# Layer 1's modulation computed in the steps of layer 0's input projection

## The reference

```
for l in range(DEPTH):                                   # DEPTH = 2
    mod = silu(cond) @ mod_w[l] + mod_b[l]               # (1024) x (1024, 6144), for two cond vectors
    sh_a, sc_a, g_a, sh_f, sc_f, g_f = split(mod, 6)
    hn = rms_norm(x, norm_mix_g[l]) * (1 + sc_a) + sh_a
    out = hybrid_mixer(hn) if l == 0 else rec_mixer(hn)  # both begin with a projection of hn
    x = x + g_a * out
    hn = rms_norm(x, norm_ffn_g[l]) * (1 + sc_f) + sh_f
    x = x + g_f * expert_choice_ffn(hn, ...)             # 16 experts, each takes its top tokens
```

## Time and profile before

| what | value |
|---|---|
| median of 3 runs | 4371.22 us (4369.33 to 4372.78) |
| profiled execution, its own time | 4360.98 us |
| its span, first to last instruction | 4359.0 us |
| mean granted clock of TensorE | 0.955 |
| busy in the span: TensorE, VectorE, ScalarE, POOL | 3926.4, 1756.0, 1102.8, 184.5 us |
| stage: `hyena_in`, i = 1 to 3 and its end | about 132.7 to 320 |
| stage: route of layer 0 | 1065.4 to 1166 |
| stage: route of layer 1 | 3351.1 to 3439 |

### The profile page before, as it was taken

How to read it: one execution, slowest core, us unless ns; L and a number is a source line. 1 busy time by engine, 2 the same in 40 slices (tenths; PEclk the granted TensorE clock), 3 DMA queues, 4 the chain that set the end, 5 groups by cost and what they waited for, 6 DMA issues and landing times. The chain is left out here.

```text
span 4359.0 us, 55904 instructions
## 1 busy us (share of the span) xinstructions
PE 3926.4 (90%) x23853; PEld 3152.1 (72%) x23853; DVE 1756.0 (40%) x2865; ACT 1102.8 (25%) x2095; POOL 184.5 (4%) x203
## 2 busy tenths in 40 slices
PE   7999979998499999997999999999687399999995
PEld 4544545553299999996888888888543399999995
DVE  3325457733611111111377887888832511111112
ACT  3110135422011110111354455454422001011111
POOL 1000000000000000000000000000000000000000
PEclk8999999999699999999999999999898699999998
DMA  5311010024978888885101001100224388888884
GB/s 182 106 72 70 16 49 1 1 73 153 312 238 258 264 258 264 256 259 155 41 27 33 28 29 30 32 17 19 98 78 145 115 255 257 263 258 259 257 260 158
DMA packets 515926, 615.14 MB, mean 141 GB/s; under 512 B 16474, under 2 KB 466700, under 8 KB 512992
## 3 DMA queue, kind: packets, MB, share of 16 engines
q1 hardware_dynamic: 492480, 525.18, 37.3%
q0 software_dynamic: 19872, 75.69, 6.3%
q10 hardware_dynamic: 3328, 10.71, 0.6%
HBM read 558.36 MB, written 53.17 MB: 140 GB/s over the span
## 5 line engine op out<-in xcount | busy, mean ns | idle before, releaser
L1671 PEld LDWEIGHTS moe_pgu<-step_hnT,mw_w 128*128 128x128 f32 x8192 | 1117.3, 191 | 16.5 <-issue 16.5
L1671 PE MATMUL moe_pgu<-step_hnT,mw_w 128*128 128x160 f32 x8192 | 1125.0, 300 | 3.4 <-ACT step_hnT L1711 3.4
L1735 DVE TENSOR_TENSOR moe_hT<-moe_sg,moe_pgu 128x160 f32<-128x160 f32 x256 | 82.1, 321 | 1027.4 <-PE moe_pgu L1671 972.0
L1683 PE MATMUL moe_pol<-mw_w,moe_hT 128*128 128x256 f32 x2048 | 457.5, 381 | 2.3 <-DVE moe_hT L1735 1.0
L1922 PE MATMUL rec_pz<-step_hnT,rec_w 128*128 128x256 f32 x1920 | 424.5, 380 | 3.5 <-ACT l_zc L1994 1.9
L1683 PEld LDWEIGHTS moe_pol<-mw_w,moe_hT 128*128 128x128 f32 x2048 | 383.2, 190 | 59.0 <-DVE moe_hT L1735 9.9
L1722 ACT ACTIVATE moe_sg<-moe_pgu 128x160 f32<-128x160 f32 x256 | 77.6, 303 | 1317.8 <-PE moe_pgu L1671 1317.8
L1922 PEld LDWEIGHTS rec_pz<-step_hnT,rec_w 128*128 128x128 f32 x1920 | 362.7, 191 | 52.0 <-ACT l_zc L1994 2.3
L1926 PE MATMUL rec_pz<-rec_w,step_hnT 128*128 128x256 f32 x1280 | 288.1, 384 | 15.1 <-ACT rec_zg L1997 15.1
L1926 PEld LDWEIGHTS rec_pz<-rec_w,step_hnT 128*128 128x128 f32 x1280 | 243.9, 193 | 50.6 <-ACT rec_zg L1997 17.9
L1952 PE MATMUL rec_pg<-rec_ring 128*128 128x128 f32 x1600 | 196.5, 281 | 47.1 <-DVE rec_AT L2249 19.7
(11 more groups left out here) (367 smaller groups left out, 4414.8 us busy)
## 6 DMA issues: line engine op xcount, KB each, us to landing
mw_w<-in_moe_w_gu SPq DMA_DIRECT2D x256, 1024.0 KB, 10.6
mw_w<-in_moe_w_down SPq DMA_DIRECT2D x128, 1024.0 KB, 13.0
mw_w<-in_mod_w SPq DMA_DIRECT2D x24, 1024.0 KB, 14.3
rec_w<-in_r_w_in SPq DMA_DIRECT2D x40, 512.0 KB, 4.0
late_w<-in_mod_w POOLq DMA_DIRECT2D x16, 1024.0 KB, 6.7
scratch_xm<-op_x ACTq DMA_DIRECT2D x20, 512.0 KB, 2.6
scratch_xn<-op_xn POOLq DMA_DIRECT2D x20, 512.0 KB, 5.4
mod_w<-in_mod_w SPq DMA_DIRECT2D x8, 1024.0 KB, 16.5
```

What stands on the lines that cost most here:

```text
L1671: m = nc.tensor.matmul(pgu[2 * (f % 2) + part][:, :], w[:, j, k, (f % 2) * P:(f % 2 + 1) * P], ring[:, k, e % 8, :], start=(k == 0), stop= ...
L1683: m = nc.tensor.matmul(pol[q // 2][:, (q % 2) * SW:(q % 2 + 1) * SW], hT[:, k, 0:CL], w[:, 8 + q, k, :], start=(k == 0), stop=(k == KD - 1))
L1735: nc.vector.tensor_tensor(hT[:, f, :], sg[:, f % 2, :], pgu[2 * (f % 2) + 1][:, :], ALU.mult).then_inc(multiplied, 1)
```

## The change

`LATE` becomes five thirds: the two of layer 0 and the three of layer 1, 40 steps. They are spread over all 27 calls of i = 1 to 3, one or two behind each call. There are two accumulators (`late[0]`, `late[1]`) in place of one, and three PSUM buffers for the projection in place of four. A third's transposes (`late_columns`) stand behind calls 8, 14, 20 and 26 and at the end; VectorE adds biases and copies columns between tiles; POOL loads each third's bias and stores each third. `LayerModulation` and everything that belongs to it leaves the route, with the wait of expert 0's weights for it.

```diff
-LATE = [(g, k) for g in (1, 2) for k in range(KD)]
+LATE = [(0, 1), (0, 2), (1, 0), (1, 1), (1, 2)]
+NLATE = KD * len(LATE)
+LATE_CALLS = 27
...
-    NPS, NTR, NZ = 4, 3, 3
+    NPS, NTR, NZ = 3, 3, 3
...
-            sp.wait_ge(late_used, len(LATE))
+            sp.wait_ge(late_used, NLATE)
...
         def _(pool):
+            def store(q):
+                layer, g = LATE[q]
+                pool.wait_ge(row_ready, q + 1)
+                for j in range(4):
+                    dst = S["mod_dram"][layer].rearrange("c (g j n) -> j c g n", j=4, n=512)[j][:, g]
+                    pool.dma_start(dst, row[32 * j:32 * j + 2, q % 2, :]).then_inc(stored, 16)
+
             pool.wait_ge(late_zero, 1)
...
+            for q, (layer, g) in enumerate(LATE):
+                if q >= 2:
+                    pool.wait_ge(row_ready, q - 1)
+                load_mod_bias(pool, A, layer, brow[:, q % 2:q % 2 + 1, :], g, 1, bias_in[q % 2])
+                for k in range(KD):
+                    n = KD * q + k
+                    if n >= 2:
+                        pool.wait_ge(late_used, n - 1)
+                    pool.dma_start(mod_w[:, n % 2, :, :].rearrange("p j n -> p (j n)"),
+                                   A["mod_w"][layer, k * P:(k + 1) * P, g * 2048:(g + 1) * 2048]).then_inc(late_in[n % 2], 16)
+                if q:
+                    store(q - 1)
+            store(len(LATE) - 1)
+            pool.wait_ge(stored, 64 * len(LATE))
...
             def modulate(n):
-                g, k = LATE[n]
+                q, k = divmod(n, KD)
                 pe.wait_ge(late_in[n % 2], 16 * (n // 2 + 1))
                 if k == 0:
                     pe.wait_ge(late_zero, 2)
-                    if g > 1:
-                        pe.wait_ge(row_ready, g - 1)
+                    if q >= 2:
+                        pe.wait_ge(col_out, q - 1)
...
+            def late_columns(q):
+                pe.wait_ge(row_ready, q + 1)
+                for n in range(4):
+                    m = nc.tensor.transpose(late[q % 2][:, n * P:(n + 1) * P], row[:, q % 2, n * P:(n + 1) * P], S["ident"][:, :])
+                m.then_inc(col_tr, 1)
...
-                    if i and g == 2:
-                        for n in (6 * (i - 1) + 2 * part, 6 * (i - 1) + 2 * part + 1):
-                            if n < len(LATE):
-                                modulate(n)
-                        if part == 0:
+                    if i:
+                        call = 9 * (i - 1) + m
+                        for n in range(NLATE * call // LATE_CALLS, NLATE * (call + 1) // LATE_CALLS):
+                            modulate(n)
+                        if call % 6 == 2 and call >= 8:
+                            late_columns((call - 8) // 6)
+                        if part == 0 and g == 2:
                             transposes(i - 1)
             transposes(3)
...
+            late_columns(len(LATE) - 1)
...
-                if tile == 6:
-                    add_bias(0)
-                elif tile == 10:
-                    add_bias(1)
+                if tile in (5, 7, 9, 11):
+                    columns((tile - 5) // 2)
+                if tile in (4, 6, 8, 10, 11):
+                    add_bias((tile - 3) // 2)
+            columns(len(LATE) - 1)
...
-            if mod:
-                mod.load_weights(sp)
-
             for j in range(8):
-                if mod and j % 4 == 0:
-                    sp.wait_ge(mod.w_used, 4 * (MOD_RING + j // 4 + 1))
                 load_expert(sp, A, layer, expert_w, expert_w_in, j, 0)
...
-            if mod:
-                pe.wait_ge(copied, 1)
-                for g in range(MOD_G):
-                    mod.multiply(pe, g)
             pe.wait_ge(picked, 1)
...
-            if mod:
-                for g in range(MOD_G):
-                    mod.add_bias(dve, g)
-                mod.columns(dve)
```

More of the change, by code:

```diff
@@ L540, in hyena_in @@
         pst = [ps(f"pst{i}", [P, 512]) for i in range(NTR)]
-        late = ps("late", [P, 512])
+        late = [ps(f"late{i}", [P, 512]) for i in range(2)]
         mm, z_ready, z_used, v_steps, u_ready, tr, tr_used, zeroed = (
@@ L717, in scale, with add_bias, columns @@
                     nc.vector.tensor_scalar(x(t), x(t), rstd[:, t:t + 1], None, ALU.mult).then_inc(scaled, 1)
-            def add_bias(g):
-                if g == 0:
-                    dve.wait_ge(bias_in, 16 * 8)
-                dve.wait_ge(late_used, KD * (g + 1))
-                nc.vector.tensor_tensor(row[:, g, :], late[:, :], brow[:, g, :], ALU.add).then_inc(row_ready, 1)
+            def add_bias(q):
+                dve.wait_ge(bias_in[q % 2], 16 * 8 * (q // 2 + 1))
+                dve.wait_ge(late_used, KD * (q + 1))
+                if q >= 2:
+                    dve.wait_ge(stored, 64 * (q - 1))
+                nc.vector.tensor_tensor(row[:, q % 2, :], late[q % 2][:, :], brow[:, q % 2, :], ALU.add).then_inc(row_ready, 1)
+            def columns(q):
+                layer, g = LATE[q]
+                dve.wait_ge(col_tr, q + 1)
+                columns_of(nc, S, layer, g, late[q % 2]).then_inc(col_out, 1)
+                if (layer, g) != (0, 1) and (layer, g) != (1, 1):
+                    dve.wait_ge(col_out, q + 1)
+                    gains_of(nc, S, layer, 0 if g == 0 else 1)
             normed(0)
             nc.vector.memset(brow[:, :, :], 0.0).then_inc(late_zero, 1)
-            nc.vector.memset(late[:, :], 0.0).then_inc(late_zero, 1)
+            nc.vector.memset(late[0][:, :], 0.0)
+            nc.vector.memset(late[1][:, :], 0.0).then_inc(late_zero, 1)
             for g in (1, 2):
@@ L1416, in load_expert, with route @@
     sp.dma_start(w[:, j, :, :], src.rearrange("(k p) n -> p k n", p=P)).then_inc(w_in[j], 16)
-def route(nc, A, S, tag, hnT, layer, idx, idx_four, gates, early, expert_w, expert_w_in, next_modulation=False):
+def route(nc, A, S, tag, hnT, layer, idx, idx_four, gates, early, expert_w, expert_w_in):
     with ExitStack() as ctx:
@@ L1496, in _ @@
             nc.scalar.activation(aff[:, :, :], aff[:, :, :], ACT.Exp).then_inc(exped, 1)
-            if mod:
-                mod.load_bias(act)
-                mod.store(act)
         @block.vector
```

123 lines of the change are left out of this document (5 added, 118 removed).

## The result

The changed kernel takes **4405.83 us** (median of 4 runs, 4396.21 to 4407.55), the kernel before 4370.27 (4 runs): ratio 1.0076, 95% interval 1.0059 to 1.0093. Measured once more, beside other runs, it takes 4402.36 (4 runs, 4391.90 to 4407.71) against 4370.23 (8 runs): 1.0079, 1.0063 to 1.0096. So it is **slower by 32 to 36 us**. The forecast was slower by 20.8, 4392.0, with a range from 4379 to 4402: the direction was right, the size and the range were not.

A forecast was written before the change was run, and what follows sets the result against it. TensorE bounds layer 0's input projection, VectorE's top-k search its route. 26.5 + 1.5 + 6.5 + 0 - 13.7 = +20.8 us on 4360.98 gives 4381.8; with 10.2 to the median, 4392.0 us, range 4379 to 4402.

The forecast's parts named there:

- End of the stage: End of layer 0's input projection: last third's stores land about when the gains end, so 0, at most +1 us.
- The ring: Two-slot ring of modulation weight loads in the projection: some steps wait for their load, +6.5 us, bounds 0 and +20.
- The steps: 24 more modulation steps in the input projection: 0.855 us per step plus 0.43 entry and exit per group, +26.5 us.
- the columns: Four sets of four transposes now issued inside the projection's loop: +1.5 us, bounds 0 to 3.3.
- signs of being wrong: In the projection: load waits over 12 us, single-step groups other than 1.29 us, or the convolution waiting for cv_fwd.
- rival C: In the projection, single-step groups cost as much as pairs: 38.7 instead of 26.5, total +33 us, 4404; chance 0.05.
- rival A: In the projection, group entry is free and no load wait occurs: total +6.6 us, 4377.8; chance 0.10.
- D: Added projection steps fit into time in which TensorE does nothing: total -13.7 us, 4357.5; chance 0.03.
- The route: Layer 0's route: modulation work between the search's end and experts' first gather goes, -13.7 us, bounds 13 and 14.5.
- Rival B: In the projection, weight loads land later than 5.2 us and steps wait more: total +34 us, 4405; chance 0.15.
- From the profile to the median: Whole kernel: the median run, 4371.22, lies 10.2 us above the profiled execution; added to the forecast.

The follow-up runs named there:

- experiment 1: The change with the last third's stores issued by SP, GpSimd waiting only for the first four thirds' stores: 4394.61 us, 1.0054 of the kernel before.
- kernel 10: The change with both its bias loads and the last third's stores issued by SP instead of GpSimd: 4390.16 us, 1.0043 of the kernel before.
- (6): The kernel before with its four row stores issued by SP instead of GpSimd, also waiting for the last tile of u: 0.9998 of the kernel before.
- experiment 2: The change without 38 of its 40 modulation weight loads in the projection: 4387.84 us, 1.0043 of the kernel before.
- experiment 8: The change with its 40 bias loads issued by SP instead of GpSimd: 1.0068 of the kernel before.
- experiment 3: The kernel before without layer 1's modulation products, columns and gate rows taken from the first layer's: 4354.70 us, 0.9968 of the kernel before.

## Why the prediction was wrong, point by point

- **End of the stage: "0, at most +1". This is the step that failed.** It measured +7.3 us in both profiles of the change. The working put the stores' landing (at some 319.4 on the old clock) level with the old end at 319.5 and took landing as the end of it. The landing was right within the stage's own times: stores issued 351.26 to 353.26, landed 354.31, gains over at 354.10. But an engine has left a stage only when it has arrived, and GpSimd arrives 0.45 us + 0.081 per transfer after its last landing. The forecast had the stores' landing level with the gains, so any time for leaving was exposed in full. The trace of before had that time in view, at the end of layer 0's experts:

```profile
2044.96 1.33 POOL L1629 DMA_INDIRECT scratch_xm<-moe_oc,step_idx  x1 [3.28 <-DVE moe_oc L1745]
2054.21 3.87 SPq L456 DMA_DIRECT2D n_x<-scratch_xm  x8
```

The last store is issued by 2046.29 and has landed at 2048.49, and the next stage's first instruction comes at 2054.21. I never compared the two, since in the stage that I read GpSimd's last store was at 294.36, 24 us ahead of the end.
- **The convolution's first products:** no term; +2.7 us in the first profile of the change, +3.0 in the second (6.34 and 6.69 us). The cost is the clock's: the products take 3.65 us and half the time for which TensorE is still granted 0.50 while they run. Low until 369.01 with the first product at 363.57, that is 2.72, measured 2.69; in the second profile until 369.58 from 363.45, 3.07 against 3.04; in experiment 1 until 364.61 from 360.38, 2.12 against 2.10. In the kernel before and in kernel 10 the clock is back at 1.00 before the first product, at 318.32 and 351.30, and nothing is lost. What decides when it is back stays open: the length of the gap does not, with 3.65 us after 12.9 (before) and 3.64 after 11.5 (kernel 10), but 5.75 after 11.7 (experiment 1) and 5.34 after 13.3 (6).
- **The ring: +6.5.** Measured +10.7 with what hangs on it (experiment 2): a term mis-sized, with the mechanism right. Calls 9, 15, 18 and 24 came as forecast: 2.63, 0.63, 0.99 and 1.09 against 3, 0.5, 1.0 and 1.0, and no first step of a third waited. Call 12 waited 0.44 and not 0. Call 6 waited 2.43 and not 1.0. The load that it waits for, issued at 176.81, lands 6.7 us after its issue and not 5.2 (6.6 in the second profile). Ahead of it GpSimd issues the eight bias rows of the next third (168.44 to 172.29), of which the forecast asked only whether they delay the third's first step; they put off the load before to 172.28. With the bias rows on SP (experiment 8) the late load takes 5.6 us and call 6 waits 1.31, so they are part of it. How they do it is not shown: that the load before is still under way is not enough, since the next load, issued at 181.43 with this one still under way, landed after 5.3. And the forecast had no price for what a wait of over 2 us does to the clock: 1.7 us in the call behind it; in the second profile of the change, 1.7 us behind call 9's wait of 3.21 instead, and nothing behind call 6's of 2.35.
- **The steps, +26.5, and the columns, +1.5:** measured 26.0 together (experiment 2), 2.0 under the forecast. Singles cost 1.21 and pairs 2.07, 0.08 less each than forecast, times 26 groups: that is the 2.0. Of the forecast's signs of being wrong this is one, a single at other than 1.29, if by little. So the entry is 0.35 us and not 0.43; rival C (pairs and singles alike) and rival A (no entry, 18.8) are both refuted, and so is D, the steps in idle time. The Trainium skill's rule that a change of tiling mode drains TensorE ("TensorEngine Tiling (Array Packing)", Key Properties) fits these rows, a fixed 0.35 us per visit; no run here tells a drain from another cost of entry.
- **The route, -13.7:** measured -13.6 in the change, -13.4 in experiment 3. Right.
- **Rival B** (loads late, +34) gives 4405 and so comes nearest to the measured time (C's 4404 is as near), but that would be luck, for the way is another: the waits were 8.2 us, short of the 12 at which I had written that I would be wrong. The Trainium skill's rule that was named there ("SBUF — State Buffer", SBUF: two separate sides), that VectorE can hold up GpSimd's descriptors, does not show in these rows: in the changed kernel eight late loads were issued inside VectorE's L663, and their issues took 0.62 us instead of 0.54; five of the eight landed 5.2 to 5.5 us after their issue, as loads do that were issued outside it.
- **From the profile to the median:** the 10.2 us between them, carried along unexplained, are the attention stage's two lengths. The forecast was right to keep them.

The sum by measured terms: 26.0 + 10.7 + 7.3 + 2.7 - 13.6 = 33.1, against 32 to 36 by the medians (0.8 of the 10.7 is unplaced). The forecast's 20.8 lacks the end of the stage (7.3), the convolution's head (2.7) and part of the ring (4.2), and has 2.0 too much for steps and columns: 12.2 in all.

## What to carry to other kernels

When a change moves an engine's last transfer nearer to the end of its stage, look in the trace for the same engine ending another stage, and read how long the next stage's first instruction waits behind the landing; give GpSimd's last transfers to another queue if it is the last to arrive, and count its transfers. Here both experts stages of the kernel before end so, with 4.7 us between GpSimd's last landing and the last arrival; what could be saved there was not tested. Before moving work from one stage into another to get rid of a tail, look at what the tail consists of: here twelve two-partition additions became three and went under the search, which gave 10 us where the move cost 32 to 36. Compare profiles stage by stage, since a stage that the change does not touch can differ by more than the change is worth.

## What the runs showed of the hardware

- GpSimd's arrival at the end of a stage comes 2.68, 4.68, 5.28, 5.45, 8.55 and 8.57 us after its last landing, with 28, 52, 60, 62, 100 and 100 transfers issued in the stage. Counted from the landing, these lie on one line to within 0.05 us; counted from the end of the last issue, the best line misses by up to 0.7, which speaks for the landing. What GpSimd does in it no row shows.
- The attention stage's first 80 us run at a mean granted clock of 0.91 or about 0.7, and the stage takes 324 or 331.5 to 335.5 us, in different executions of the same kernel. What decides it was not tested.
- Behind a wait of 2.43 us TensorE was granted 0.50 for 3.4 us, which cost 1.7 us. In the other execution of the same kernel nothing fell behind a wait of 2.35 us in the same place, and 1.7 us were lost behind the next, of 3.21. Experiments 1, 8 and 10 show one such stretch each, behind waits of 2.34, 3.08 and 2.76; behind 2.63 (the first profile's second wait) and 3.10 (experiment 1's) nothing fell. So a wait of this size may or may not cost up to 1.7 us more, and its length alone does not decide it.
- The first products of the convolution were longer by half the time for which the granted clock was still 0.50 while they ran: 2.69, 3.04 and 2.10 us with 5.44, 6.13 and 4.23 us of it.
